# Adaptive-norm modulation blocks taken out of the delta branch's merge and put one stage on, the last of them among the first down projection

## The reference, cut to what matters

```
mod = silu(c) @ w_ada + b_ada                       # 6 x 2048 wide
sh1, sc1, g1, sh2, sc2, g2 = split(mod, 6)
a = rmsnorm(x, ng0) * (1 + sc1) + sh1
proj = a @ w_in
... two recurrent branches, o_hg and o_gdn ...
merged = sigmoid(gate_a) * (o_hg @ w_out_hg) + sigmoid(gate_b) * (o_gdn @ w_out_gdn)
mix = merged @ w_o
h = x + g1 * rmsnorm(mix, ng1)
a = rmsnorm(h, ng2) * (1 + sc2) + sh2
y = h + g2 * rmsnorm(square(relu(a @ w_up)) @ w_down, ng3)
```

## Time and profile before

| | us |
|---|---|
| median of three runs | 3591.82 (3589.3 to 3592.94) |
| the profiled execution's own time | 3585.92 |
| span of its trace | 3584.0 |
| PE busy in the span | 3487.8 |
| DVE busy | 2255.7 |
| ACT busy | 1798.6 |
| S_WA on PE | 811.0 to 956.2 |
| S_WB1 on PE | 1607.4 to 1745.2 |
| S_WB2 on PE | 2402.5 to 2566.2 |
| S_WO on PE | 2566.2 to 2711.6 |
| first round: up, down on PE | 2736.8 to 2849.5, 2849.5 to 2951.4 |

### The profile page before, as it was taken

The page is one execution under the profiler, slowest core; times in us unless marked ns, Lnnn a source line. Parts: engine busy times, 40 slices in busy tenths (PEclk is TensorE's granted clock), DMA queues, the critical chain, the costliest instruction groups (busy, mean ns, idle before and its releaser), DMA issues.

```text
span 3584.0 us, 76959 instructions
## 1 busy us (share of the span) xinstructions
PE 3487.8 (97%) x24605; PEld 3175.2 (89%) x24605; DVE 2255.7 (63%) x4307; ACT 1798.6 (50%) x3735; POOL 845.1 (24%) x995
## 2 busy tenths in 40 slices
PE   9999999999999999999999999999998999999998
PEld 2599999998889989998899999997787999999998
DVE  2467667646677777776677777546666545555555
ACT  1345555455545455555555555454565435444454
POOL 2122222211145544451244544411100000000000
PEclk9999999999999999999999999999998999999999
DMA  8655555568844434448643434468874555555554
GB/s 287 208 148 159 151 156 150 148 187 260 239 110 116 113 108 119 120 115 265 184 129 108 117 108 116 130 194 269 242 229 129 166 164 162 166 162 166 162 164 139
DMA packets 884544, 588.06 MB, mean 164 GB/s; under 512 B 23426, under 2 KB 816036, under 8 KB 884164
## 3 DMA queue, kind: packets, MB, share of 16 engines
q1 hardware_dynamic: 857828, 510.50, 49.7%
q0 software_dynamic: 26624, 76.41, 7.5%
HBM read 545.83 MB, written 40.99 MB: 164 GB/s over the span
## 4 chain that ended last, share of the span: by engine, by line
PE 90%; DVE 4%; issue 2%; DMA 2%; ACT 1%; DVEq 0%; ACTq 0%; POOL 0%; SPq 0%; POOLq 0%
PE acc L602 23%; PE acc L604 21%; PE acc L603 21%; PE acc L574 3%; PE bank L792 2%; PE bank L805 2%; PE bank L842 2%; PE bank L826 1%; DVE wlo L1521 1%; ACT whi L1027 1%; PE bank L614 1%; DMA raw<-in_w_out_gdn 1%; PE bank L615 1%; DMA raw<-in_w_ada 1%; PE bank L863 1%
## 5 line engine op out<-in xcount | busy, mean ns | idle before, releaser
L1521 DVE TENSOR_TENSOR wlo<-raw,whi 128x512 fp32r<-128x512 f32 x1799 | 1305.0, 743 | 853.3 <-ACT whi L1027 842.7
L1027 ACT ACTIVATE whi<-raw 128x512 fp32r<-128x512 f32 x1799 | 1096.5, 627 | 872.0 <-PE acc L604 828.9
L602 PE MATMUL acc<-ahi,whi 128*128 128x288 f32 x4112 | 1288.9, 313 | 14.0 <-DVE alo L2035 8.4
L603 PE MATMUL acc<-alo,whi 128*128 128x288 f32 x4112 | 1215.7, 296 | 0.0
L604 PE MATMUL acc<-ahi,wlo 128*128 128x288 f32 x4112 | 1212.0, 295 | 0.0
L602 PEld LDWEIGHTS acc<-ahi,whi 128*128 128x128 f32 x4112 | 775.7, 189 | 36.7 <-issue 25.7
L603 PEld LDWEIGHTS acc<-alo,whi 128*128 128x128 f32 x4112 | 776.8, 189 | 13.3 <-issue 11.5
L604 PEld LDWEIGHTS acc<-ahi,wlo 128*128 128x128 f32 x4112 | 776.2, 189 | 0.0
L602 PE MATMUL acc<-ohi,whi 128*128 128x288 f32 x1792 | 536.5, 299 | 12.8 <-DVE wlo L1521 8.6
L603 PE MATMUL acc<-olo,whi 128*128 128x288 f32 x1792 | 530.6, 296 | 0.0
L604 PE MATMUL acc<-ohi,wlo 128*128 128x288 f32 x1792 | 528.9, 295 | 0.0
(11 more groups left out here) (431 smaller groups left out, 4327.5 us busy)
## 6 DMA issues: line engine op xcount, KB each, us to landing
raw<-in_w_in SPq DMA_DIRECT2D x386, 512.0 KB, 4.1
raw<-in_w_ada SPq DMA_DIRECT2D x192, 512.0 KB, 4.7
raw<-in_w_up SPq DMA_DIRECT2D x128, 512.0 KB, 4.1
raw<-in_w_down SPq DMA_DIRECT2D x128, 512.0 KB, 4.0
raw<-in_w_out_gdn SPq DMA_DIRECT2D x64, 512.0 KB, 4.9
raw<-in_w_o SPq DMA_DIRECT2D x34, 512.0 KB, 4.6
raw<-in_w_out_hg SPq DMA_DIRECT2D x32, 512.0 KB, 5.2
g_S<-in_state_gdn POOLq DMA_DIRECT2D x32, 512.0 KB, 6.8
```

The costliest lines, as they stand in the source:

```text
L602: mm(bank[:, 0:T], whi[:, s, r, :], hi[:, kt, :], start=(kt == 0), stop=False, skip_group_check=True)
L603: mm(bank[:, 0:T], whi[:, s, r, :], lo[:, kt, :], start=False, stop=False, skip_group_check=True)
L1027: f(whi[:, s], raw[:, r], ACT.Copy).then_inc(sg["hi_made"], 1)
L1521: tt_(wlo[:, s], raw[:, r], whi[:, s].bitcast(F32), SUB).then_inc(sg["lo_made"], 1)
```

## The change

The list of mixed stages is changed. S_WB2 becomes a plain stage, S_WO now makes sc2, and the first down projection (S_DOWN0) becomes mixed and makes g2. All 16 blocks remain, with the same instructions. The calls of `mod_add` and `mod_scaled` move with them, and since the feed-forward is no longer one regular row of pieces, positions in it come from a helper, `ff_pos`.

```diff
-    MIXED = (S_WA, S_WB1, S_WB2, S_WO)
+    S_DOWN0 = S_FF + KT
+    S_FF1 = S_FF + 2 * KT
+    MIXED = (S_WA, S_WB1, S_WO, S_DOWN0)
...
+        def ff_pos(g, n):
+            return pos(S_FF, n, 2) if isinstance(g, int) and g == 0 else pos(S_FF1, n + (g - 1) * KT, 2)
...
# SP
-            mixed_loop(sp, mixed(wgdn, KT), S_WB2)
+            loop(sp, pair(wgdn, KT, 0), S_WB2, 2, KT // 2)
             mixed_loop(sp, mixed(wo, 0), S_WO)
-            with sp.Fori(0, FG) as g:
+            loop(sp, pair(wup, 0, 0), S_FF, 2, KT // 2)
+            mixed_loop(sp, mixed(wdown, 0), S_DOWN0)
+            with sp.Fori(1, FG) as g:
...
# PE
-            mixed_loop(pe, mixed(ohi, olo), S_WB2)
+            loop(pe, plain(ohi, olo), S_WB2, 2, KT // 2)
...
+            with pe.Fori(0, KT // 2) as n:
+                for k in range(2):
+                    products(ff_pos(0, n), k, ahi, alo, ready=("b_lo", 0, 1))
+            mixed_loop(pe, mixed(ohi, olo, ready=("f_lo", EARLIER, 1)), S_DOWN0)
+            with pe.Fori(1, FG) as g:
...
# ACT
-            mixed_loop(act, both, S_WB2)
+            loop(act, both, S_WB2, MIXED_SLABS, MIXED_BLOCKS)
...
-            down_hi(0)
+            mixed_loop(act, only_hi, S_DOWN0)
...
# DVE, in the merge's body
-                    if k == MIXED_SLABS - 1:
-                        mod_add(at, n)
...
-            mod_scaled(S_WB2, 4, 2, True)
...
             tt_(samples(mix, 0, KT), samples(mix, 0, KT), mod_samples(2, 0, KT), MUL).then_inc(sg["w_t2"], 1)
+            mod_scaled(S_WO, 4, 2, True)
             dve.wait_ge(sg["w_rs"], 1)
...
-            mod_scaled(S_WO, 5, 3, False)
...
+            def first_down(at, n):
+                for k in range(MIXED_SLABS):
+                    down(at, 2 * n, k, (lambda: mod_add(at, n)) if k == MIXED_SLABS - 1 else None)
...
-            downs(0)
+            mixed_loop(dve, first_down, S_DOWN0)
+            mod_scaled(S_DOWN0, 5, 3, False)
```

More of the change, by code:

```diff
@@ L367, in hybrid_layer @@
         mod_rows = {S_WA: gC[0:2 * NC].rearrange("p a c -> p (a c)"), S_WB1: gns[0:2 * NC].rearrange("p a c -> p (a c)"),
-                    S_WB2: ytok[0:2 * NC].rearrange("p k a c -> p (k a c)"), S_WO: ytok[0:2 * NC].rearrange("p k a c -> p (k a c)")}
+                    S_DOWN0: ytok[0:2 * NC].rearrange("p k a c -> p (k a c)"), S_WO: ytok[0:2 * NC].rearrange("p k a c -> p (k a c)")}
         def mixed_block(slab, n):
             return ADA_BLOCKS + MIXED.index(slab) * MIXED_BLOCKS + n
+        def ff_pos(g, n):
+            return pos(S_FF, n, 2) if isinstance(g, int) and g == 0 else pos(S_FF1, n + (g - 1) * KT, 2)
         def repeat(eng, body, count):
@@ L490, in _ @@
             loop(sp, pair(win, 0, GATE_B + 6 * P), S_GB1, 2, (KT - 6) // 2)
-            mixed_loop(sp, mixed(wgdn, KT), S_WB2)
+            loop(sp, pair(wgdn, KT, 0), S_WB2, 2, KT // 2)
             mixed_loop(sp, mixed(wo, 0), S_WO)
-            with sp.Fori(0, FG) as g:
+            loop(sp, pair(wup, 0, 0), S_FF, 2, KT // 2)
+            mixed_loop(sp, mixed(wdown, 0), S_DOWN0)
+            with sp.Fori(1, FG) as g:
                 with sp.Fori(0, KT // 2) as n:
-                    at = pos(S_FF, n + g * KT, 2)
+                    at = ff_pos(g, n)
                     for k in range(2):
@@ L498, in _ @@
                 with sp.Fori(0, KT // 2) as n:
-                    at = pos(S_FF, n + g * KT + KT // 2, 2)
+                    at = ff_pos(g, n + KT // 2)
                     for k in range(2):
@@ L946, in _ @@
             last.then_inc(sg["w_ss"], 1)
-            with pe.Fori(0, FG) as g:
+            with pe.Fori(0, KT // 2) as n:
[3 more added lines that the diff above has]
+            with pe.Fori(1, FG) as g:
                 with pe.Fori(0, KT // 2) as n:
-                    at = pos(S_FF, n + g * KT, 2)
                     for k in range(2):
-                        products(at, k, ahi, alo, ready=("b_lo", 0, 1))
+                        products(ff_pos(g, n), k, ahi, alo)
                 with pe.Fori(0, KT // 2) as n:
-                    at = pos(S_FF, n + g * KT + KT // 2, 2)
                     for k in range(2):
-                        products(at, k, ohi, olo, ready=("f_lo", EARLIER + g * KT, 1))
+                        products(ff_pos(g, n + KT // 2), k, ohi, olo, ready=("f_lo", EARLIER + g * KT, 1))
             pe.wait_ge(sg["w_ln"], 2)
@@ L1404, in down_hi @@
                     for k in range(2):
-                        slab_hi(pos(S_FF, n + g * KT + KT // 2, 2), k)
+                        slab_hi(ff_pos(g, n + KT // 2), k)
             up_slab(0, 0, 0, made=1)
@@ L1415, in _ @@
             with act.Fori(0, KT // 2) as n:
-                at = pos(S_FF, n + FG * KT - KT // 2, 2)
+                at = ff_pos(FG - 1, n + KT // 2)
                 for k in range(2):
@@ L1971, in _ @@
             dve.wait_ge(sg["g_stored"], 16 * GJ)
-            mixed_loop(dve, both, S_WB2, apart=1)
+            loop(dve, both, S_WB2, MIXED_SLABS, MIXED_BLOCKS, apart=1)
             merged_lo(MIXED_BLOCKS - 1, MIXED_SLABS - 1)
-            mod_scaled(S_WB2, 4, 2, True)
             def clear_sum(v):
@@ L2060, in up, with down @@
                         up_slab(g, n, k)
-            def down(at, n, k):
+            def down(at, n, k, added=None):
                 slab_lo(at, k)
+                if added:
+                    added()
                 dve.wait_ge(sg["piece_used"], at.slab_end(k))
@@ L2071, in downs @@
                     for k in range(2):
-                        down(pos(S_FF, n + g * KT + KT // 2, 2), n, k)
+                        down(ff_pos(g, n + KT // 2), n, k)
+            def first_down(at, n):
+                for k in range(MIXED_SLABS):
+                    down(at, 2 * n, k, (lambda: mod_add(at, n)) if k == MIXED_SLABS - 1 else None)
             up_slab(0, 0, 0, made=1)
@@ L2089, in last_down @@
                 for k in range(2):
-                    down(pos(S_FF, n + FG * KT - KT // 2, 2), n, k)
+                    down(ff_pos(FG - 1, n + KT // 2), n, k)
             repeat(dve, last_down, KT // 2)
-            at = pos(S_FF, KT // 2 - 1 + FG * KT - KT // 2, 2)
+            at = ff_pos(FG - 1, KT - 1)
             for k in range(2):
```

## The result

The changed kernel takes 3563.3 us (median of six runs, 3559.6 to 3565.4) where the kernel before took 3592.2 us beside it (3589.3 to 3594.3). The ratio is 0.9918, 95% interval 0.9908 to 0.9928: 0.8% faster, 28.9 us. Forecast were 24.5 us and a time of 3567.3 in a range of 3561 to 3581.

The account below looks back on a forecast made before the run. TensorE was taken to bound the kernel (busy 3487.8 of 3584.0 us), losing 29.5 us in the merge. Terms -59.4 + 34.9 = -24.5 us took the 3591.8 median to 3567.3, range 3561 to 3581.

Parts of the forecast that it names:

- (a): Merge (S_WB2) loses its blocks and becomes plain: 163.8 to 104.4 us, minus 59.4, with 2 us kept for feeders.
- (b): First down projection gains the blocks: 101.9 to 136.8 us, +34.9, of which 2.5 is its own loss.
- The 2 us kept for late feeders: Plain merge: allowance for DVE and ACT, `tin` and DMA feeding PE late; 2 us, bounds 0 and 8.
- At 0.89 these three pairs take 13.6 instead of 12.8 us, +2.4: Plain merge's three slab pairs with x need DMA share 0.95; capped at 0.89, the highest stage share, they lose 2.4 us.
- (c): S_WO keeps four blocks with other columns, same instructions: nothing.
- (d): `mod_scaled` of sc2 moves behind S_WO, hidden with 0.5 us to spare; that of g2 behind first down, at most 0.3.
- (e): Two more loops on each engine, with code to load and other position arithmetic: nothing, bound 2 us.
- a late split: Merge before: weight loads waited for DVE's `wlo`, from DVE's load and DMA demand of 312 GB/s; 29.5 us over PE's pace.
- Nothing is lost anywhere: Rival: neither plain merge nor first down loses anything, -29.5 us, 3562.3; included in the 0.72 forecast case.
- The blocks cost the first down as much as the merge: Rival: first down loses 29.5 us to the blocks as the merge did, 3593.8, no change; chance 0.06.
- the merge's slab is set by its own chain: Rival: the merge's slab stays at 9.41 us without blocks, +21.7 us, 3613.5; chance 0.04.
- Half bound by its feeders: Rival: late `tin`, x and weights keep 8 to 18 us of the merge's loss, 3574 to 3584; chance 0.16.

Follow-up runs that it names:

- run 2: Kernel before, branch tiles loaded only for the first two slabs and used for all 16; merge 162.1 us (163.7 before), ratio 0.9991.
- run 3: Kernel before, each load of `w_ada` in the merge brings one piece instead of two; merge 155.3 us (163.7 before), ratio 0.9973.
- run 7: Kernel before, complete, ACT rounds a merged slab behind its first split of the next one; merge 156.4 us (163.7 before), ratio 0.9982.
- run 4: Kernel before, two of DVE's three merge steps on 4 columns instead of 288; merge 159.1 us (163.7 before), ratio 0.9982.
- run 9: Kernel before, branch tiles loaded once and ACT's rounding one split later (run 2 and run 7 together); merge 144.9 us, ratio 0.9943.
- run 5: Changed kernel, POOL begins a pair's branch loads only after PE used 2 pieces of the next pair; merge 131.5 us, ratio 1.0002 to kernel before.
- run 10: Kernel before, half the bytes of `w_ada` in the merge and ACT's rounding one split later (run 3 and run 7 together); merge 150.1 us, ratio 0.9958.
- run 6: Changed kernel, POOL begins a pair's branch loads only after PE used 4 pieces of the next pair; merge 140.9 us, ratio 1.0027 to kernel before.

## Why the prediction was right

Of the 28.7 us by stages, forecast were 24.5. The 4.2 between them are 1.9 in (a), 1.4 in (b) and 0.9 in stages that were put at nothing, all of one sign.

*Yardsticks.* 0.133 us for a matmul, 6.4 for a slab, 134.3 for a mixed stage: the merge now takes 102.40 for 102.4.

*(a) The merge.* Forecast -59.4, measured -61.3. The 2 us kept for late feeders were not needed. Each feeder came out near its count. DVE and ACT: the first split behind a slab ended 3.5 to 3.8 us behind it, and 4.4 in the last pair, forecast 3.7 with 4.8 for the limit. `tin`: forecast 0.7 early to 0.6 late, measured up to 0.86 late, with no loss to PE. DMA: forecast share 0.85 for the stage and 0.95 for the three pairs with x, measured 0.86 and these:

```profile
2434.10:2446.90 12.80, 12.80 (x98) 12.80 (x97) 8.65 (x16) 5.47 (x10) 4.44 (x8) 1.00 0.97 279
2446.90:2459.70 12.80, 12.80 (x98) 12.80 (x97) 8.66 (x16) 5.52 (x10) 4.45 (x8) 1.00 1.01 285
```

Two pairs in a row filled the DMA engines at 279 and 285 GB/s and PE lost nothing. The step that was mis-sized is "At 0.89 these three pairs take 13.6 instead of 12.8 us, +2.4": the highest share seen in a stage is not a limit. The engines ran full for 25 us and PE lost nothing, though a weight load took up to 8.3 us to land there. The 282 GB/s of the earlier trace rows, at which the rows had put full engines, was near (285) over a pair of slabs, but not over less: the busiest 5 us within the second pair ran at 337.

```profile
2453.60:2458.60 5.00, 5.00 (x40) 5.00 (x39) 3.63 (x7) 2.41 (x5) 0.26 (x1) 1.00 1.09 337
```

The Trainium skill ("DMA: Bandwidth & Descriptors", Specifications) has 358 GB/s for HBM. No pair came near it, and yet the 2 us vanished, as the prediction said they would by that page.

*(b) The first down.* Forecast +34.9, measured +33.5: its own loss is 1.6 us, not 2.5, and the stage of before was 102.4, not 101.9. Those 1.6 lie mostly ahead of the 9th weight and the 10th block piece, behind the burst of four block pieces.

*(c), (d), (e).* S_WO and the norms changed by 0.3 us. `mod_scaled` was hidden with 0.8 us to spare (0.5 forecast). The new loops cost nothing.

*What bounded the merge before.* The prediction named a late split, and as reasons DVE's load and the rate of 312 GB/s that a mixed merge would want. Part of this was right: the loads are one limit. But eased alone they gave 1.6 us (run 2, all of it the clock's) and 8.4 (run 3, 5.0 without the clock). The other limit, at least as large (7.3 in run 7, none of it the clock's), is one the prediction didn't name, the lead of three pieces that is worth less time where pieces are short (runs 4, 7, 9). It did not matter for the forecast, since a plain merge has neither.

*The rivals.* "Nothing is lost anywhere", which the forecast's range took in, was the nearest in time: 3562.3, and 3563.3 was measured. It was wrong by the 1.6 us of the first down, and by the stages that changed by 0.9. "The blocks cost the first down as much as the merge" and "the merge's slab is set by its own chain" fell: 1.6 us and a slab of 6.4. "Half bound by its feeders" did not come true, but was nearer than its chance of 0.16 with 8 to 18 us said: run 5 shows that 1.6 us more on POOL cost 29. The prediction priced a landing 1 us beyond the worst at 4 us for the stage; it left out that the tiles would then meet the next load of weights, and that PE's gaps bring the low clock. It took landing times from the kernel before and did not ask when the weight loads would go out beside the tiles. That they stayed 1.3 to 1.5 us behind them was luck.

Open stays how the 15.8 us that run 10 still loses divide between the landings beside x and the rest: 7.1 lie at the seven places, 3.8 are PE's wait for `mod_out`, and 1.7 are the clock. Not tried was a load order that keeps the branch tiles ahead of the weights by force.

## What to carry to other kernels

A lead of so many pieces is a lead in time only by the pieces' cost on the consumer: count it in us at the place where the chain begins, with the short pieces that lie in it. When work is moved out of a stage, ask what that stage loses by itself, not what the work costs: the blocks cost 34 us wherever they were, but the merge gave back 61. When a stage has two limits close together, cures tried singly can show little (1.6 and 7.3 us) and together much (18.8), so an experiment with one cure can't clear a cause. Read the clock beside each: a fall more or less was as large as the smallest of these gains. And a stage that runs at its floor may be a microsecond from a cliff: delay its loads on purpose to see.

## What the runs showed of the hardware

- The third branch tile of a set (144 KB each, software queue) took 3.4 us to land when the 512 KB load of the hardware queue went out 1.5 us behind the first of its set, 5.1 when it went out 0.1 us ahead, and 4.8 when it went out 0.1 us behind. With no such load near (run 6) it took 2.6 to 3.8. So 1.4 us in the order of issue made 1.4 us in the landing.
- The DMA engines ran at a share of 0.97 and 1.01 for 12.8 us each, with rows of 512 bytes for the weights, at 279 and 285 GB/s, and for 5 us at 337, without any loss to PE.
- Seven gaps of PE of 1.9 to 3.3 us in 131.5 us (run 5) cost 18.8 us by themselves and some 10 more by the lower clock, which came behind five of them; seven of 3.0 to 4.1 us in 140.9 us (run 6) cost 24.0 and some 15.
